# Stores of the pointwise and attention results begun from ScalarE's queue instead of SyncE's, in a one-core encoder layer

## The reference

```
h = RMSNorm(x);  a, gate, q, k, v = split(h @ w_in)
u = a * sigmoid(gate)
c = silu(LayerNorm(causal depthwise conv of width 31 over u)) @ w_pw      # 512 channels, "pointwise"
z = RMSNorm(q) . RMSNorm(k) / 8                                          # 8 heads of 64
A[t,s] = sigmoid(z[t,s]) * prod over s<j<t of (1 - sigmoid(z[t,j]))      # strictly causal
o = A @ v
x = x + concat(c, o) @ w_out
x = x + relu(RMSNorm(x) @ w_ff1)^2 @ w_ff2
```

## Time and profile before

| | us |
|---|---|
| median of 3 runs | 2774.53 |
| lowest and highest of them | 2772.41, 2780.32 |
| span of the profiled execution | 2777.2 |

### The profile page before, as it was taken

How to read it: one execution, slowest core, us unless ns; L and a number is a source line. 1 busy time by engine, 2 the same in 40 slices (tenths; PEclk the granted TensorE clock), 3 DMA queues, 4 the chain that set the end, 5 groups by cost and what they waited for, 6 DMA issues and landing times. The chain is left out here.

```text
span 2777.2 us, 37645 instructions
## 1 busy us (share of the span) xinstructions
PE 2687.2 (97%) x14000; PEld 2270.3 (82%) x14000; DVE 1663.9 (60%) x2621; ACT 1069.5 (39%) x2146; POOL 453.3 (16%) x462
## 2 busy tenths in 40 slices
PE   8988899999999999999999999999999999999999
PEld 6757778788887887788888797778888887998998
DVE  6996767577763576377775368627888842222122
ACT  4434524455552122355553212335666631221211
POOL 2122210022210010032221102103333310000000
PEclk9999999999999999999999999999999999999999
DMA  9795797697769568455554747845355456443532
GB/s 330 255 349 188 237 355 266 259 336 253 256 218 375 214 233 282 184 209 185 168 187 165 284 186 237 291 163 190 118 181 191 150 188 248 187 177 122 212 152 95
DMA packets 262048, 616.21 MB, mean 222 GB/s; under 512 B 23217, under 2 KB 159409, under 8 KB 213741
## 3 DMA queue, kind: packets, MB, share of 16 engines
q1 hardware_dynamic: 261869, 613.80, 61.8%
HBM read 444.79 MB, written 168.94 MB: 221 GB/s over the span
## 5 line engine op out<-in xcount | busy, mean ns | idle before, releaser
L2020 PE MATMUL ps<-h2T_hi,w_s 128*128 128x512 f32 (+2 forms) x1312 | 469.2, 358 | 7.9 <-DMA w_s<-w_scratch 3.9
L2022 PE MATMUL ps<-h2T_hi,w_s 128*128 128x512 f32 (+2 forms) x1312 | 458.3, 349 | 0.0
L1174 POOL TENSOR_TENSOR beta<-beta,stay 128x512 f32<-128x512 f32 (+3 forms) x328 | 313.0, 955 | 889.5 <-DVE stay L1859 853.4
L2021 PE MATMUL ps<-h2T_lo,w_s 128*128 128x512 f32 (+2 forms) x1312 | 457.9, 349 | 0.0
L1929 DVE TENSOR_TENSOR resid<-ps,resid 128x512 f32<-128x512 f32 x256 | 174.6, 687 | 261.3 <-PE ps L2285 260.6
L1451 ACT ACTIVATE stay<-ps 128x512 f32<-128x512 f32 (+3 forms) x328 | 174.8, 533 | 347.2 <-PE ps L2221 227.1
L2283 PE MATMUL ps<-w_s,hid_hi 128*128 128x512 f32 x768 | 308.3, 401 | 0.0
L2284 PE MATMUL ps<-w_s,hid_lo 128*128 128x512 f32 x768 | 299.9, 390 | 0.0
L2285 PE MATMUL ps<-w_s,hid_hi 128*128 128x512 f32 x768 | 299.8, 390 | 0.0
L1526 ACT ACTIVATE ps<-ps 128x512 f32<-128x512 f32 (+1 forms) x160 | 81.3, 508 | 542.7 <-PE ps L2022 542.7
L2020 PEld LDWEIGHTS ps<-h2T_hi,w_s 128*128 128x128 f32 x1312 | 248.0, 189 | 38.3 <-DMA w_s<-w_scratch 4.0
(11 more groups left out here) (217 smaller groups left out, 5179.1 us busy)
## 6 DMA issues: line engine op xcount, KB each, us to landing
w_s<-w_scratch SPq DMA_DIRECT2D x282, 1024.0 KB, 7.5
w_scratch<-w_s SPq DMA_DIRECT2D x94, 1024.0 KB, 8.3
w_raw<-in_w_ff SPq DMA_DIRECT2D x64, 512.0 KB, 5.7
a_k<-k_scratch SPq DMA_DIRECT2D x80, 256.0 KB, 3.8
a_v<-v_scratch SPq DMA_DIRECT2D x80, 256.0 KB, 4.0
a_q<-q_scratch SPq DMA_DIRECT2D x64, 256.0 KB, 4.4
w_raw<-in_w_in SPq DMA_DIRECT2D x20, 512.0 KB, 7.7
mix_scratch<-ohl SPq DMA_DIRECT2D x66, 128.0 KB, 3.0
```

The costliest lines, as they stand in the source:

```text
L1174: nc.gpsimd.tensor_tensor(v[0:q.r, 0:n], v[0:q.r, 0:n], stay_of(q.z)[0:q.r, 1:n + 1], ALU.mult).then_inc(s_a, 1)
L2020: nc.tensor.matmul(out, w[0], x[0], start=start, stop=False)
L2021: nc.tensor.matmul(out, w[0], x[1], start=False, stop=False)
L2022: return nc.tensor.matmul(out, w[1], x[0], start=False, stop=stop)
```

## The change

Both stores leave SyncE's stream and are begun by ScalarE, with the same sizes and semaphores. The store of pw stands, in the front, right behind ScalarE's cast of the same m. In the windows it stands behind hid_hi of the same slot, but for the last m, where it stands right behind the cast. The store of an attention result stands at the head of att_later, one step after ScalarE's cast to ohl, where SyncE had it two steps after.

```diff
@@ SyncE: att, front, window
-                q = att_piece(c, step, VALUES + 3)
-                if q and q.out:
-                    sp.wait_ge(o_lo, q.o + 1)
...
-            def store_pw(c, ev):
...
-                sp.wait_ge(pw_lo, CB * c + ev + 1)
-                sp.dma_start(mix_d[:, m, :, c * CHUNK + q0:c * CHUNK + q0 + w].rearrange("v p t -> p v t"),
-                             pwo[:, ev % 2, :, 0:w].bitcast(F32)).then_inc(pw_st[ev % 2], 16)
...
@@ ScalarE: front
                     if m is not None:
                         pw(0, m)
+                        store_pw(0, m)
...
+            def store_pw(c, m):
+                pieces = conv_pieces(c)
+                for n, (a, q0, w) in enumerate(pieces):
+                    ev = len(pieces) * m + n
+                    act.wait_ge(pw_lo, CB * c + ev + 1)
+                    act.dma_start(mix_d[:, m, :, c * CHUNK + q0:c * CHUNK + q0 + w].rearrange("v p t -> p v t"),
+                                  pwo[:, ev % 2, :, 0:w].bitcast(F32)).then_inc(pw_st[ev % 2], 16)
+
+            def store_out(c, step):
+
+                q = att_piece(c, step, VALUES + 2)
+                if q and q.out:
+                    act.wait_ge(o_lo, q.o + 1)
...
             def att_later(c, step):
+                store_out(c, step)
                 q = att_piece(c, step, TURN)
...
@@ ScalarE: window
                         if m is not None:
                             pw(n, m)
+                        if m == CB - 1:
+                            store_pw(n, m)
...
                         nc.scalar.copy(hid_hi[x][:, j, s0:s0 + w], bank).then_inc(f_hi, 1)
+                    m = pw_part(n, s - 1) if n < NC else None
+                    if m is not None and m < CB - 1:
+                        store_pw(n, m)
                     for step in steps[:1]:
                         att_later(n, step)
```

More of the change, by code:

```diff
@@ L948, in att @@
                     load_running()
-                q = att_piece(c, step, VALUES + 3)
-                if q and q.out:
-                    sp.wait_ge(o_lo, q.o + 1)
[L952 to L960, removed]
-            def store_pw(c, ev):
-                pieces = conv_pieces(c)
-                m, n = ev // len(pieces), ev % len(pieces)
-                a, q0, w = pieces[n]
-                sp.wait_ge(pw_lo, CB * c + ev + 1)
-                sp.dma_start(mix_d[:, m, :, c * CHUNK + q0:c * CHUNK + q0 + w].rearrange("v p t -> p v t"),
-                             pwo[:, ev % 2, :, 0:w].bitcast(F32)).then_inc(pw_st[ev % 2], 16)
             def load_mix_part(c, b, v):
@@ L1001, in front @@
                     weights(TICK["win", -1, t])
-                    m = pw_part(0, t - 1)
-                    if m is not None:
-                        store_pw(0, m)
                     if t >= att_past(0) + 2 and t in MIX_AT:
@@ L1032, in window @@
                             att(n, step)
[L1033 to L1037, removed]
                         if n == NC - 1 and s == 20:
@@ L1435, in pw @@
                     nc.scalar.copy(pwo[:, ev % 2, 0, 0:w], ps[:, T_BANK + ev % 2, 0:w]).then_inc(pw_hi, 1)
+            def store_pw(c, m):
[9 more added lines that the diff above has]
+                    act.wait_ge(o_lo, q.o + 1)
+                    if q.kind:
+                        for v in range(2):
+                            act.dma_start(mix_d[v, CB:KD, :, SEQ:SEQ + DEC].rearrange("b p t -> p b t"),
+                                          ohl[q.o % 2][:, v, :].bitcast(F32).rearrange("p (b t) -> p b t", t=DEC)).then_inc(o_st[q.o % 2], 16)
+                    else:
+                        me = q.head % 2 * HD
+                        col = c * CHUNK + 2 * P * q.p
+                        act.dma_start(mix_d[:, CB + q.head // 2, me:me + HD, col:col + 2 * P].rearrange("v p t -> p v t"),
+                                      ohl[q.o % 2][me:me + HD, :, :].bitcast(F32)).then_inc(o_st[q.o % 2], 16)
             def att_sigmoids(c, step):
```

## The result

| | before | after |
|---|---|---|
| median (lowest to highest) | 2775.32 us (2772.41 to 2780.32) | 2804.62 us (2798.5 to 2806.91) |
| ratio, 95% interval | | 1.0098 (1.0085 to 1.011) |
| span of the profiled execution | 2777.2 us | 2802.4 us |

The kernel became 1% slower, where I had forecast no difference: 29 us by these medians, 27 us by the ratio, which is that to 2777.5 us, the median of the 25 runs of before that stand beside e1 to e4. The profiled pair shows 25.2 us.

A forecast was written before the change was run, and what follows sets the result against it. TensorE, busy 97% of the span, was taken as the bound, so only its gaps could move. Terms -5.8 - 3.9 + 0.7 + 5.9 + 3 + 1.5 + 0.5 = +1.9 us on the median gave about 2776.5 us, range 2765 to 2789.

The forecast's parts named there:

- pw in chunks 0 to 2: Front and windows 0 and 1: front free; third store's issue ahead of the fourth pwo cast adds 0.37 us twice, +0.7.
- The late weight load in window 1: Window 1, near 1169: without the pwo stores SyncE loads earlier, so TensorE's 3.88 us gap goes, -3.9.
- pw in chunk 3: Chunk 3: casts of m=1 and m=3 wait for stores behind hid_hi to land, +2.9 and +3.0, together +5.9 us.
- 13.4, if loads get in the way: Upper bound for pw in chunk 3: twice the longest pwo landing of 6.7 us.
- A 7.2 us stall in the front: Front, near 311: ohl store 9 on ScalarE's queue ends ScalarE's stall, of which TensorE feels 5.80 us; -5.8.
- attention in the front: Chunk 0, 16 ohl stores: issues and waits for ohl's low part on ScalarE, +3 us, bounds 0 and 9.9.
- my bound of 302.4: Front: latest time ohl store 9 may land to cost nothing, 309.61 less 7.22.
- Attention in chunks 1 to 3: ohl stores on ScalarE: +0.5 us in chunks 1 and 2, +1.5 in chunk 3 through delays reaching TensorE.
- My slower rival: Chunk 3's attention: ScalarE's waits reach TensorE, up to 22 us instead of 1.5, so 2797; chance 0.12.
- The store doesn't pass the loads: Front: by strict reading of shared DMA engines the 5.8 us stay, 2782.3 us; chance 0.08.
- The signs of being wrong: Changed profile: aT_lo waits over 20 us, a ScalarE issue well over 0.7 us, or the 7.2 us stall still standing.

The follow-up runs named there:

- e1: Changed kernel with the 20 pwo stores and their waits given back to SyncE, only the 66 ohl stores on ScalarE; 2777.06 us, ratio to before 0.9998.
- e4: Changed kernel with ScalarE's wait for the landing of pwo stores moved from ahead of a relu to just ahead of the first aT_hi cast; 2782.95 us, 1.0017.
- e10: Changed kernel, but in window 2 SyncE holds the same slot's weight load until the stores of m=0 and m=2 have landed; 2800.21 us, 1.0086.
- e2: Changed kernel with the 66 ohl stores given back to SyncE, only the 20 pwo stores on ScalarE; 2804.51 us, ratio to before 1.0095.
- e7: Changed kernel with window pwo stores right behind their casts, the landing wait just ahead of the first aT_hi cast, ohl stores on SyncE; 2768.77 us, 0.9976.
- e5: Changed kernel, but SyncE still waits for pwo's low parts where its stores stood, so weight loads begin no earlier than before; 2796.15 us, 1.0071.
- e9: e5 with the windows' store of the last m given back to SyncE, which begins it ahead of the weight loads; 2789.68 us, 1.0054.
- e3: Changed kernel with each pwo store in the windows right behind its own cast instead of behind hid_hi; 2782.37 us, 1.0015.

## Why the prediction was wrong

By the profiles the change costs 25.2 us where the sum had 1.9. Of the 23.3 us between them 18.0 are the first term below, and 7.8 the third; the late weight load gave 2.9 back.

**"pw in chunks 0 to 2": failed.** I priced it at two issues, +0.7, and wrote of the third store only that it stands ahead of the fourth cast. I had written in the description that ScalarE waits for all of pw_st one slot before the attention, and then left that wait out of the sum, since no row of before shows it: there the last store lands in 2.8 and 3.0 us, under the wait for TensorE. It measured +7.7 us in window 0 and 4.89 + 5.68 / 2 accounts for it (gap, and half of the 5.68 us that TensorE is then busy at the lower clock); in window 1 it measured 11.0, and 8.00 + 5.88 / 2 accounts for that. I named no work that covers this landing, so I did not see that the change takes the cover away. The two issues that I did price cost nothing: the fourth pwo cast starts 0.48 us behind the hid_hi cast in before (551.61, 552.09) and in after (549.84, 550.32; 1166.18, 1166.66), with the issue beginning together with hid_hi, and TensorE's gap at the fourth cast of window 1 is 0.51 us in both.

**"The late weight load in window 1", -3.9: right, and undersized.** Its gap is gone. What it was worth is 6.8: 3.9 for the gap and half of 5.75 us at the lower clock. The row of after shows 6.7 gained up to the matmul of 1176 and 11.0 lost behind it, +4.3 together.

**"pw in chunk 3", +5.9: the mechanism was right, the size not.** It measured +13.7. The landing was 5.7 and 6.0 us, not 2.8, so the two gaps grew by 5.25 and 5.56 us instead of 2.9 and 3.0. The rest is clock: 5.34 + 3.92 us busy at the lower level against 3.05 in before, half of the difference is 3.1, and the sum is 13.9. I had named the case, "13.4, if loads get in the way" (that it is so near 13.7 is luck: two landings of 6.7 us and no clock, against 10.8 of gaps and 3.1 of clock), and chosen the median of all 20 stores instead, which says nothing of the four that start with a load. e10 takes the load away and finds my mechanism and nearly my size: the gaps grow by 2.30 and 2.27 us instead of 2.9 and 3.0, as the store's issue starts together with the hid_hi cast (1871.34 both in after) and not behind it.

**"A 7.2 us stall in the front" (-5.8) and "attention in the front" (+3): together about 0.** The gap of 5.80 is gone, but not for my reason. The store, begun 1.2 us earlier, took 9.8 us against 12.9 and landed at 305.30, past my bound of 302.4; no wait is left because ScalarE itself comes to the cast of result 11 only at 306.20. But TensorE is 2.3 us later by 299, in stretches where ScalarE begins stores, and gets another gap of 1.90 near 321. From 268 to 369 the changed kernel gains 0.1 us. e2 and e7, which leave ohl's stores on SyncE and keep the gap (6.0 and 6.1 us), lose 0.1 us there. e1 and e2 say the same with whole runs.

**Attention in chunks 1 to 3, +0.5 and +1.5: right to within 2 us.** In e1, which moves ohl's stores alone, the stages behind the front show +0.7, 0.0, -0.1, +0.1, +0.1 and 0.0 us. My slower rival, 2797 by these waits, would have come near the measured time for a wrong reason; e1 rules it out.

**The rivals.** "The store doesn't pass the loads" was asked of one store of ohl whose gain it might cancel. The question belonged to every moved store that someone waits for. That rival leant on the Trainium skill, "DMA: Bandwidth & Descriptors", section "Issuing engines are not separate DMA queues": DMAs interleave on the same DMA engines, and another issuer saves only the time of starting. The runs agree with the interleaving (7.8 us beside eight loads, e5) and add what it means for a small store: it loses the place ahead that SyncE's queue gave it (3.1 us, e9). Its section "Queues, rings and completion order" has the DMA engines take turns between queues packet by packet. The counts of e5 agree, 177 packets against 178.

**The signs of being wrong: none showed.** I had named waits for aT_lo over 20 us (8.6), an issue well over 0.7 us (0.58) and the stall standing (gone). All three watched attention and the issues; none watched the landing of the pwo stores.

## What to carry to other kernels

When a transfer moves to another engine's queue, list who waits for its landing, also where no wait shows today, and price the landing beside the transfers that start at the same moment, not by a median. A small store ahead of large loads was well off in their queue here; in another it shared with them by packets, the smaller packets getting fewer bytes. And freeing the first queue can make them start earlier still. Price a gap of TensorE, where the granted clock falls, by its length and half of the work that it then does at the lower clock.

## What the runs showed of the hardware

- A 512 KB store landed in 3.0 us (before) and 3.1 us (e9) with 1 MB loads right behind it in the same queue; in a queue of its own in 7.8 us with loads started 0.1 us later (e5), and in 11.1 us behind seven loads, the last begun 1.0 us before it (after).
- Two queues with work got as many packets each (177 and 178 in 4 us, e5), 2 KB and 7.5 KB long.
- A store's first packet moved 0.9 us after its start with no load ahead (e10), and 3.3 us after it with a 1 MB load begun 1.2 us before (after, chunk 3).
- Stores of one queue follow each other: behind the one of 11.1 us the next took 15.0, and 10.8 without it (e3).
- Passing is partial: the 11.1 us store landed at 1177.24, ahead of three of the seven loads begun before it. Store 9 of ohl landed in 9.8 us in ScalarE's queue and 12.9 in the loads'; two weight loads were begun ahead of it in the first case and four in the second, so the two aren't quite alike.
- After gaps of TensorE of 3.2 to 8.5 us came stretches of 3.4 to 10.3 us at 1.2 GHz, which begin in the gap or right behind it. After the gap of 2.36 us behind chunk 2's attention came one in after and none in before: that is the +1.6 us in the table, which no store explains. Half of the busy time in them, with the gaps, accounts for TensorE's losses in windows 0 and 1 and chunk 3 to within 0.3 us.
